# Latent attention scores as a 64-row and a 32-row product, value product one pair later

## The reference

```python
MLA_HEADS, MLA_NOPE, MLA_ROPE, MLA_V = 16, 64, 32, 64
q = rms_norm((rms_norm(q_a) @ w_q_b).reshape(B, n, 16, 64 + 32), q_norm)
q_nope, q_rope = split(q, [64]); q_rope = apply_axial_rope(q_rope)
k_nope, v = split((rms_norm(kv_a) @ w_kv_b).reshape(B, n, 16, 64 + 64), [64])
k_nope = rms_norm(k_nope); k_rope = apply_axial_rope(rms_norm(k_r))  # one k_rope for all heads
score = (q_nope . k_nope + q_rope . k_rope) * 96 ** -0.5
o = softmax(score over 1280 keys) @ v
y = (o * silu(g)) @ w_out
```

## Time and profile before

| | us |
|---|---|
| median of 3 runs | 3589.13 (3585.70 to 3591.74) |
| the profiled execution | 3590.77, its span 3588.9 |
| first key product of the layer to the end of half 0's last value product | 2663 to 3067 |
| same of half 1 | 3067 to 3472 |
| PE busy, share of the span | 95% |

### The profile page before, as it was taken

The page is one execution under the profiler, slowest core; times in us unless marked ns, Lnnn a source line. Parts: engine busy times, 40 slices in busy tenths (PEclk is TensorE's granted clock), DMA queues, the critical chain, the costliest instruction groups (busy, mean ns, idle before and its releaser), DMA issues.

```text
span 3588.9 us, 54379 instructions
## 1 busy us (share of the span) xinstructions
PE 3409.3 (95%) x22925; PEld 1936.5 (54%) x22925; DVE 1653.7 (46%) x2637; ACT 1144.3 (32%) x1927; POOL 505.6 (14%) x489
## 2 busy tenths in 40 slices
PE   8999999998899989899999999989999999899999
PEld 4466655654333334445655555655555666466654
DVE  2555666634311138334555454453225555455542
ACT  1334343311111125333333333342214444244430
POOL 0222222311000014111010011001112000200000
PEclk9999999999899999999999999999999999999999
DMA  3022111214799899200000000031100000000001
GB/s 115 25 66 72 66 41 50 91 59 149 298 355 382 308 377 361 51 18 19 1 19 18 19 19 12 1 133 39 57 0 13 1 1 14 24 1 1 1 27 68
DMA packets 115386, 302.61 MB, mean 84 GB/s; under 512 B 13142, under 2 KB 55446, under 8 KB 101958
## 3 DMA queue, kind: packets, MB, share of 16 engines
q1 hardware_dynamic: 78470, 231.91, 17.8%
q10 hardware_dynamic: 29760, 42.05, 3.2%
q0 software_dynamic: 6912, 25.17, 1.9%
HBM read 345.71 MB, written 55.10 MB: 112 GB/s over the span
## 4 chain that ended last, share of the span: by engine, by line
PE 86%; DVE 7%; DMA 2%; ACT 2%; issue 1%; POOL 1%; SPq 1%; DVEq 0%; ACTq 0%; POOLq 0%
PE ps L2816 11%; PE ps L451 9%; PE ps L2262 8%; PE ps L2291 8%; PE ps L3528 7%; PE ps L1832 6%; PE ps L2834 5%; PE ps L3800 3%; PE ps L3209 3%; PE ps L1268 3%; PE ps L1852 3%; PE ps L3481 2%; PE ps L2500 2%; PE ps L3198 1%; PE ps L3189 1%
## 5 line engine op out<-in xcount | busy, mean ns | idle before, releaser
L2816 PE MATMUL ps<-sb 128*128 128x512 f32 x960 | 464.6, 603 | 19.6 <-ACT sb L2174 10.9
L2262 PEld LDWEIGHTS ps<-sb 128*128 128x128 f32 x2624 | 288.5, 141 | 303.7 <-ACT sb L2270 130.0
L2262 PE MATMUL ps<-sb 128*128 128x128 f32 x2624 | 418.0, 282 | 19.4 <-DVE sb L2278 9.5
L2270 ACT ACTIVATE sb<-ps 128x512 f32<-128x512 f32 x336 | 200.1, 597 | 715.0 <-PE ps L2262 715.0
L2236 ACT ACTIVATE sb<-ps,sb 128x1280 f32<-128x1280 f32 (+1 forms) x288 | 353.2, 1231 | 130.7 <-DVE sb L2229 112.2
L2278 DVE COPY sb<-ps 128x512 f32<-128x512 f32 x320 | 219.9, 688 | 376.7 <-PE ps L2262 376.2
L451 PE MATMUL ps<-sb 128*128 128x512 f32 x704 | 347.3, 613 | 4.5 <-DMA sb<-in_w_in 2.9
L3528 PE MATMUL ps<-sb 96*128 96x512 f32 (+1 forms) x768 | 332.2, 525 | 9.0 <-DVE sb L3585 7.2
L2291 PEld LDWEIGHTS ps<-sb 128*64 128x64 f32 x5248 | 287.6, 138 | 70.7 <-issue 40.4
L2291 PE MATMUL ps<-sb 128*64 128x128 f32 x5248 | 322.2, 277 | 3.3 <-DVE sb L2278 3.1
L2057 POOL TENSOR_TENSOR sb<-sb 128x1 f32<-128x1 f32 (+3 forms) x114 | 131.9, 1158 | 1056.1 <-DVE sb L2053 1056.0
(11 more groups left out here) (379 smaller groups left out, 4345.6 us busy)
## 6 DMA issues: line engine op xcount, KB each, us to landing
sb<-in_exp_gate SPq DMA_DIRECT2D x65, 1024.0 KB
sb<-in_exp_up SPq DMA_DIRECT2D x65, 1024.0 KB
sb<-in_exp_down SPq DMA_DIRECT2D x65, 1024.0 KB
sb<-in_l_w_mod ACTq DMA_DIRECT2D x12, 2048.0 KB, 16.6
d_ys<-sb ACTq DMA_DIRECT2D x32, 512.0 KB, 4.2
d_ys<-sb SPq DMA_DIRECT2D x64, 256.0 KB
sb<-d_x SPq DMA_DIRECT2D x32, 512.0 KB, 3.9
sb<-in_w_in SPq DMA_DIRECT2D x22, 512.0 KB, 4.5
```

The costliest lines, as they stand in the source:

```text
L2262: ins = k.pe.e.transpose(k.bank(bank)[:, 128 * j:128 * j + 128], self.Pb[g % 2][:, 1280 * b + 128 * c:1280 * b + 128 * c + 128], k.f(C_ID, ...
L2270: k.act.e.activation(self.PT[:, xs[0]:xs[-1] + 1, :], k.bank(bank)[:, 0:128 * len(xs)].rearrange("p (j t) -> p j t", j=len(xs)), ACT.Copy) ...
L2816: ins = pe.e.matmul(k.bank(5), lhs[:, kk, :], w[:, kk, 512 * half:512 * half + 512], start=kk == 0, stop=kk == 7)
```

## The change

The score of a pair is computed in two rounds that add up in PSUM. The 64-value part of the two heads is laid side by side: head A on rows 0 to 63, head B on rows 64 to 127 of `kN` and `qN`. The 32-value rotary part is repeated on the four quarters of the rows (`kR`, `qR`), so that products on different quarters can run side by side. All six products of the rotary round (`rope`) stand together, then one group of transposes, then the six of the other round (`nope`). Where two products write the same bank (A2 and B0), a semaphore orders them. The extremes are taken by one DVE kind (`max`) in four reductions instead of three. There are two buffers for the transposed weights, and the value product of pair g - 2 is cut in two halves that stand between the transposes of pair g - 1. Groups 0, 1 and 4 are now copied by ACT, 2 and 3 by DVE. The key stage turns two heads at once (4 transposes of 128 columns per chunk instead of 8 of 96), ACT alone copies them, and the rotary keys are turned once, in half 0. The query's rotary sum is written twice, and its 64-value part is scaled into a buffer of its own.

```diff
+    AT = {"A0": (0, 0, 512, 0), "A1": (0, 512, 1024, 1), "A2": (0, 1024, 1280, 0), "B0": (1, 0, 256, 2), "B1": (1, 256, 768, 2), "B2": (1, 768, 1280, 3)}
...
+        for name, out, src in (("A0", m[:, 0:1], ps[:, 0:512]), ("A2", m[:, 2:4], ps[:, 1024:1536].rearrange("p (b t) -> p b t", b=2)),
+                               ("A1", m[:, 1:2], ps[:, 512:1024])):
...
+            dve.e.tensor_reduce(out, src, AX, ALU.min).then_inc(*self.maxed.up())
...
+        dve.e.tensor_reduce(mx[:, i:i + 1], m[:, 0:3], AX, ALU.min).then_inc(*self.maxed.up())
...
+        dve.e.tensor_reduce(m[:, 4:5], ps[:, 1536:2560], AX, ALU.min).then_inc(*self.maxed.up())
...
+        dve.e.tensor_tensor(mx[:, i + 1:i + 2], m[:, 3:4], m[:, 4:5], ALU.min).then_inc(*self.maxed.up())
...
-            for h4 in range(2):
-                b = (4, 6)[h4]
-                pe.wait_ge(*free[b])
-                for j in range(4):
-                    ins = pe.e.transpose(k.bank(b)[0:96, 128 * j:128 * j + 128], k8s[c % 2][:, 4 * h4 + j, :], ident)
...
+            for j in range(4):
+                ins = pe.e.transpose(k.bank(b)[:, 128 * j:128 * j + 128], k8s[c % 2][:, 2 * j:2 * j + 2, :].rearrange("p h d -> p (h d)"), ident)
...
-        ins = pe.e.matmul(k.ps[:, 1280 * b + lo:1280 * b + hi], qT[0:96, h, :], kT[:, h, lo:hi], start=True, stop=True, skip_group_check=True)
...
+            pe.wait_ge(*st.t["exp", g - 1, 1])
...
+            ins = pe.e.matmul(k.ps[:, 1280 * b + lo:1280 * b + hi], qR[rows, p, :], kR[rows, lo:hi], start=name != "B0", stop=False, skip_group_check=True)
...
+            ins = pe.e.matmul(k.ps[:, 1280 * b + lo:1280 * b + hi], qN[rows, p, :], kN[rows, p, lo:hi], start=False, stop=True, skip_group_check=True)
...
-        elif kind == "pturn" and x[1] in (1, 2, 3):
+        elif kind == "pturn" and x[1] in (0, 1, 4):
...
+            at[0, 3] = [("mmq", hh, n + 1, 0, kk) for kk in range(3)] + [("qe", hh, n + 1, 0)]
+            at[1, 3] = [("mmq", hh, n + 1, 1, kk) for kk in range(3)] + [("qe", hh, n + 1, 1), ("qsquare", n + 1)]
+            at[2, 0] = [("qsum", n + 1)]
+            at[2, 2] = [("qscale", n + 1)]
+            at[2, 4] = [("qnorm", n + 1)]
             at[3, 2] = [("qadd", hh, n + 1)]
+            at[3, 3] = [("qturn", hh, n + 1, 0), ("qTe", hh, n + 1, 0)]
+            at[3, 4] = [("qturn", hh, n + 1, 1), ("qTe", hh, n + 1, 1)]
...
+                yield ("rope", g, ("A2", "A1", "B1", "B2", "A0", "B0"))
+            if turn:
+                yield ("pturn", g - 1, 0, not more)
             if more:
+                yield from at.get((r, 0), ())
+                if g:
+                    yield ("nope", g, ("A0", "B0", "B1", "A2", "B2", "A1"))
+                yield ("max", g)
+            if turn:
+                yield ("pturn", g - 1, 1, not more)
             if more:
+                yield ("exp", g, 0)
+                yield from at.get((r, 1), ())
+            if weigh:
+                yield ("weigh", g - 2, 0)
+            if turn:
+                yield ("pturn", g - 1, 2, not more)
+            if more:
+                yield ("exp", g, 1)
+                yield from at.get((r, 2), ())
+            if weigh:
+                yield ("weigh", g - 2, 1)
+                if g % 4 == 1:
+                    yield ("consume", hh, st.pairs[g - 2][0], g - 2)
+            if turn:
+                yield ("pturn", g - 1, 3, not more)
+            if more:
+                yield from at.get((r, 3), ())
+            if turn:
+                yield ("pturn", g - 1, 4, not more)
```

More of the change, by code:

```diff
@@ L3489, in pe_program @@
             for j in range(4):
-                ins = pe.e.transpose(k.bank(5)[0:96, 128 * j:128 * j + 128], q8[:, 4 * half + j, :], ident)
+                ins = pe.e.transpose(k.bank(5)[:, 128 * j:128 * j + 128], m.qd[:, 512 * (1 - half) + 128 * j:512 * (1 - half) + 128 * j + 128], ident)
             ins.then_inc(*turned.up())
@@ new lines, in pe_nope @@
+    def pe_nope(st, g, names):
+        n, p, _ = st.pairs[g]
+        pe.wait_ge(*t["qN", t["hh"], n])
+        for name in names:
+            b, lo, hi, _ = st.AT[name]
+            rows = slice(64 * b, 64 * b + 64)
+            if name == "A2":
+                pe.wait_ge(*st.t["B0 nope"])
+            ins = pe.e.matmul(k.ps[:, 1280 * b + lo:1280 * b + hi], qN[rows, p, :], kN[rows, p, lo:hi], start=False, stop=True, skip_group_check=True)
+            if name == "B0":
+                ins.then_inc(*st.shared.up())
+                st.t["B0 nope"] = st.shared.at
+            elif name != "B1":
+                flag = st.scored_b if name == "B2" else st.scored
+                ins.then_inc(*flag.up())
+                st.t["scored", g, name] = flag.at
@@ L3556, in act_program @@
             t["v"] = evac_a.at
-        elif kind == "qTe" and x[2]:
+        elif kind == "qTe" and not x[2]:
             act_turn_out(*x)
@@ L3737, in attention @@
         st = t["st"]
-        for g in range(-1, len(st.pairs)):
-            more = g + 1 < len(st.pairs)
+        last = len(st.pairs)
+        for g in range(last + 2):
+            more, turn, weigh = g < last, 0 <= g - 1 < last, g >= 2
             at = {}
             if more:
-                n, r, _ = st.pairs[g + 1]
+                n, r, _ = st.pairs[g]
                 at = window(hh, n)
-            for u in range(6):
-                if g < 0 and u == 2:
-                    yield from (("kturn", NTT - 1), ("kTe", NTT - 1), ("keys_end",))
-                if g >= 0 and u != 3:
-                    yield ("pturn", g, u - u // 4)
-                if more:
-                    if u == 4:
-                        yield ("exp", g + 1, 0)
-                    yield ("score", g + 1, u // 3, u % 3)
-                    yield from at.get((r, u), ())
-            if more:
-                yield ("exp", g + 1, 1)
-                yield from at.get((r, 6), ())
-            if g >= 0:
-                yield ("weigh", g)
-                if g % 4 == 3:
-                    yield ("consume", hh, st.pairs[g][0], g)
-            if more:
-                yield from at.get((r, 7), ())
@@ new lines, in attention @@
+            if more:
[11 more added lines that the diff above has]
+                yield ("pturn", g - 1, 4, not more)
+            if more:
+                yield from at.get((r, 4), ())
```

225 lines of the change are left out of this document (143 added, 82 removed).

## The result

| | before | after |
|---|---|---|
| median, us | 3588.68 (4 runs, 3585.70 to 3591.74) | 3631.60 (4 runs, 3630.88 to 3634.15) |
| the profiled execution's span | 3588.9 | 3629.6 |
| half 0 of the layer, first key product to the next half's | 403.4 | 422.4 |
| half 1 of the layer | 405.3 | 423.3 |

The changed kernel is slower: ratio 1.0118, interval 1.0104 to 1.0132. That is +43 us; forecast were +9.7, range -16 to +36. In the two profiled executions the spans differ by 40.7 us. The two halves of the layer hold 36.9 of it (808.8 us before, 845.6 after), and 3.8 lie ahead of the layer, in stages that the change doesn't touch.

What follows compares the result with a forecast made beforehand. The prediction took PE's instruction stream as the bound. Attention +18.7, starts of the halves -2 and keys -7 gave +9.7 us on 3589.13, so 3599 us; its own range was 3582 to 3616, with most rivals 3573 to 3625.

Steps and rivals of the forecast that it cites:

- The sum of a step: PE's order in a plain attention step, start to start: 10.19 us against 9.26 before, with 2.34 for the 64-row round.
- The clock falls: Rival, 4%: PE idles 0.95 us per step, so the clock partly drops to half speed; 20 us, 3619 us.
- before the first of them ... 1 us less per half: Ahead of each half's first transposes, a DVE copy is gone and two rounds replace six products: 1 us less per half.
- The rotary round: Scores on four row quarters abreast: 1.28 us for the fullest quarter plus 0.21, so 1.49 us; bounds 1.39 and 2.34.
- The rival of 9%: Rotary round runs two abreast or in program order: 2.34 us instead of 1.49, 53 us more, 3652 us; 9%.
- the 1.60 us that the prediction set beside its own number: Rotary round by the Trainium skill's 3.07x for four row tiles: 1.39 + 0.21 us, kernel 7 us slower than forecast.
- Hidden changes of shape: Rival, 19%: array shape changes, eight per step, are mostly hidden; 0.3 to 0.5 us less a step, 3568 to 3580 us.
- DVE ends last: Rival, 6%: reductions or summed rounds 0.7 us late, third copy holds the fourth group by 0.4: 25 us, 3624 us.
- The fourth group's wait: Fourth group of transposes and the wait for DVE's copy, ahead of the fifth: 1.44 us, 0.95 of it uncovered.
- A tile: Four attention steps with query work, 11.84, 10.6, 10.19 and 10.9 us: 43.5 us against 42.43, plus 1.1.
- the attention stages: From first transposes to each half's end: 342.7 us against 332.8 and 333.9, 9.9 and 8.8 more, 18.7 in all.
- Keys: Key stage, four fewer transposes per chunk: 0.45 us for eight chunks, 3.5 us per half, 7 in all; between 0 and 10.

Runs made afterwards that it cites:

- b0_first: The changed kernel with B0 ahead of A0 in the 64-row round (B0, A0, B1, A2, B2, A1); 3606.65 us, ratio 1.0043.
- filled: b0_first with useless transposes (11, 6 and 9) put where PE waits at the start of each half; 3592.96 us, ratio 1.0010.
- two_rows: The changed kernel with the rotary round on two of the four row quarters; 3687.3 us, ratio 1.0271.
- start_whole: b0_first with pair 0 of each half scored like every other pair, after the last keys are turned and copied; 3594.5 us, ratio 1.0018.
- mmq_early: The changed kernel with the next tile's three 128-row query products moved ahead of pair 0's first 64-row products; 3639.7 us, ratio 1.0135.
- full_rows: b0_first with 30 useless 128-row transposes ahead of pair 0's first 64-row products, idle time kept; 3601.8 us, ratio 1.0039.
- joined: b0_first with the value product's two halves together between the third and fourth group of transposes; 3642.8 us, ratio 1.0139.

## Why the prediction was wrong

- **The sum of a step** held, but for the 64-row round. It took the 2.34 us of the earlier trace rows, which b0_first does reach (2.35). The changed kernel pays 2.71, since one of its products waits for a signal that a longer product ahead holds back: 0.37 x 62 = 23 us. The section on the change names the semaphore between A2 and B0, and the prediction gave it no cost, neither from a row nor by a bound. This is the first step that failed, and it alone is as large as two thirds of the miss of 33 us.
- **"The clock falls", 4%**, was the right rival in the wrong place. It looked at the 0.95 us in each step, where the clock stayed at 1.00 throughout. The term that failed is "before the first of them ... 1 us less per half". It counted records and not the clock; measured were 9.2 and 8.6 us more. 7 of each are the clock: 20.1 and 19.9 us against 12.8 to 13.05 in b0_first and filled at full clock. The other 2 are the stretch itself, which is no shorter than before but longer: waits between the pieces of pair 0. Against the forecast of -2 us for both halves the starts cost 19.8 us more, nearly as much as the rounds.
- **The rotary round**: 1.50 us for 1.49 forecast, and 2.35 if two abreast (two_rows) for 2.34. The rival of 9% falls, and the 1.60 us that the prediction set beside its own number is too long.
- **Hidden changes of shape, 19%**: no. The two halves of the value product are 1.25 us each for 1.28, a group ahead of them 0.58.
- **DVE ends last, 6%**: no row shows PE behind a reduction.
- **The fourth group's wait**: 1.44 us to the fifth as forecast.
- **A tile** was forecast as 43.5 us; without the 0.37 four times it is 42.9 (44.4 in the changed kernel). Each of the first, second and fourth steps was 0.15 to 0.21 shorter than forecast. From the second rotary round to its end a half was to take 342.7 us. In b0_first it takes 337.7: of the 5.0 less 3.4 are the six whole tiles and 0.8 the first step, which the sum priced like any other although it has no value product yet (9.77 us instead of 10.6). The changed kernel takes 348.8. So the attention stages were to grow by 18.7 us, and grew by 30.8 = 18.7 + 22.2 for the rounds - 10.1 for steps priced too high.
- **The time before** held something that the forecast took over unseen: the value product at the very end of its halves took 3.73 and 4.46 us (3063.02 to 3066.75, 3467.63 to 3472.09) where the last one after takes 2.33, since the clock was low there. These 3.5 us were no part of the change.
- **Keys**: -6.3 and -5.5 us, not -3.5 each; inside its bounds of 0 to 10. In half 0 at most 1.7 us of it are a fall of the clock that this stage has in the profile of before (granted 0.60 from 2676 to 2680) and not in that of after. 2.6 us in each half are the wait for DVE's copy of the queries, which the forecast did not look at.

The miss of 33 us adds up from the profiles: +22 for the rounds, +20 for the starts, -10 for the steps, -5 for the keys, and +6 outside the layer's count (3.8 ahead of it, 2.2 between the profiled runs and the medians). That it is no larger is luck: two terms that were too dear stand against two that were missing.

Without its two faults the change is the kernel of filled: 1.0010 of the kernel before, no difference that can be told. Its steps are longer (10.12 against 9.26), as forecast, and the key stage pays it back.

## What to carry to other kernels

Where products on different rows run side by side, order them so that the one whose signal is waited for stands ahead of the longer ones, not behind them: its signal comes only when those have ended. When a stage starts after short waits of TensorE, look at the granted clock of its first 20 us: they are priced by the clock, not by the count of records. Here it paid to fill the waits (filled) or to start with whole rounds (start_whole); putting full-row products first shortened the first fall but brought no time (mmq_early, full_rows). A wait removed by a second buffer is gone only if the buffer's other user isn't next in line.

## What the hardware showed that was not expected

- A product's signal waits for the products ahead of it, on other rows too: 0.89 us from record to waiter behind a product of 512 columns, 0.43 with none ahead.
- Both records of an fp32 product need not be issued before the next product starts on other rows; so two or four abreast cost 0.22 us over the fullest quarter, 1.50 us for 2560 columns on 32 rows each.
- Idle pieces of 1.3, 0.7 and 1.1 us with work between them were enough for the clock to fall in some executions and not in others, while 0.95 us once in 10.5 us never did it in the changed kernel. After a fall it stayed low for 3.4 us under products on 96 or all rows (6.8 once, at the end of the kernel before, with two waits of 0.7 and 0.8 us around it), 6.8 to 10.2 under rounds that fill the rows with two or four products, and 17.1 (20.5 in joined) where some ran on a part of the rows alone. That the rows are the reason is the reading that fits best, not one that a run isolates.
